# Cross attention: each head's norm ahead of the next head's maxima, and four output tiles taken head by head

## The chip, the core and the metric

The kernel runs on one core of a Trainium2 chip. Its time is the time of one execution on the device, in microseconds. The median of 3 runs of the kernel before is 2040.57 us (2038.38 to 2041.07).

The engines: PE multiplies matrices and writes to eight PSUM banks of 128 x 512 fp32 values; ACT (ScalarE) and DVE (VectorE) read those banks and write to SBUF; POOL (GpSimd) does a few small things; SP issues the weight transfers.

## The reference, cut to what matters

Two encoder layers, then two layers of another kind (not touched here). An encoder layer is an FFN, a mixer, a cross attention over a memory of 256 tokens, and a second FFN. The sequence has 256 tokens, D is 1024; the cross attention has 4 heads of 256.

```python
def memory_cross_attention(xn, memn, w_q, w_kv, w_o):
    B, S, D = xn.shape
    M = memn.shape[1]
    q = (xn @ w_q).reshape(B, S, XATTN_HEADS, XATTN_HEAD_DIM)
    k, v = jnp.split(memn @ w_kv, 2, axis=-1)
    k = k.reshape(B, M, XATTN_HEADS, XATTN_HEAD_DIM)
    v = v.reshape(B, M, XATTN_HEADS, XATTN_HEAD_DIM)
    s = jnp.einsum('bshd,bmhd->bhsm', q, k, preferred_element_type=F32) * (XATTN_HEAD_DIM ** -0.5)
    p = jax.nn.softmax(s, axis=-1).astype(v.dtype)
    o = jnp.einsum('bhsm,bmhd->bshd', p, v).reshape(B, S, D)
    return o @ w_o

# in a layer
h = h + memory_cross_attention(rms_norm(h, xattn_norm[l]), rms_norm(mem, mem_norm[l]),
                               xattn_w_q[l], xattn_w_kv[l], xattn_w_o[l])
h = h + 0.5 * swiglu_ffn(rms_norm(h, ffn2_norm[l]), ffn2_w_in[l], ffn2_w_out[l])
```

## The kernel before

Everything is kept with features on the 128 partitions and the 256 tokens along the free axis, so a 1024-wide vector is 8 tiles of 128 x 256 (`h`, `xs`, `yx`, `xo`). A big product splits both operands into a high part (fp32r) and the low rest: for each 128 x 128 weight block PE does three matmuls, weight high by x high, weight high by x low, weight low by x high (L383, L386, L387). An output tile is 8 blocks, 24 matmuls, and two tiles fill one bank.

The weights come in units of 8 blocks (512 KB) in the order in which PE takes them. SP loads them into a ring of 10 slots (L488); ACT writes a unit's high part (`w_hi`, 6 slots, L1031) and DVE its low part over the ring slot (`w_lo`, L1458). `s.ahead(u)` in the code of ACT and DVE makes the splits of all units up to some units past `u` at this place of the queue: up to u + 4 on ACT and u + 3 on DVE. ACT's split of a unit also waits until PE has begun the unit five before it (`unit_begun`). For the output projection of the cross attention (units U_XO to U_XO + 7) one unit is one output tile.

The order of the work is written out by hand for each engine, and the engines meet only at semaphores: `tell(name)` adds one, `need(name, n)` waits for n. Some names share a semaphore. In the cross attention (`cross_pe`, `cross_act`, `cross_dve`) a loop over i = 0 to 5 runs the heads as a pipeline. For head i:

- PE: the projection of the queries of head i + 1 (banks 1 to 3), the scores of head i (L753, bank 4 or 5), the transposes of the probabilities of head i - 1 (L767, bank 6), and the product of head i - 2's probabilities with the values (L778, bank 7). After the loop PE waits for `xo_lo` 4 and projects the output into banks 0, 1, 2 and 7, two tiles each.
- ACT: the copy of the queries (L1250), the exponentials of head i with their sums (L1263), the copy of the turned probabilities (L1270), the high part of head i - 2's output (L1274).
- DVE: the row maxima of head i and their scaling (L1751, L1753), the norm of head i - 1 (reciprocal of the sums and two multiplications, L1758, L1762), the low part of head i - 2's output (L1767).

Then `next_act` and `next_dve` add the output to `h` (L1502, as each bank is full: `w_full`), write the high and low parts of `xs` for the next FFN (L1061, L1468), and sum the squares (L1062, L1478 to L1486). The next FFN begins with `first_pair` (L448, L452, L453), which takes k-tiles 0 to 5 of its first two output tiles and then k-tiles 6 and 7 of both.

Of the kernel before, what the change touches and what calls it, by code (L numbers as in the profile page):

```python
# [25 lines left out]
ALU = mybir.AluOpType  # L26
AF = mybir.ActivationFunctionType
AX = mybir.AxisListType.X
# [18 lines left out]
XH = 4  # L47
# [130 lines left out]
def build_program(nc, counts, arrays, out):  # L178
    with ExitStack() as ctx:
# [559 lines left out]

        def cross_pe(pe, w):  # L740
            with pe.scope("cross"):
                first_pair(pe, w, yx, 0, "q_full")
                token_sums(pe, 6, wide=False)
                for i in range(XH + 2):
                    if i + 1 < XH:
                        project(pe, w, yx, KD, i + 1, "q_full")
                    if i < XH:
                        pe.e.wait_ge(*pe.need('q', i + 1))
                        if i >= 2:
                            pe.e.wait_ge(*pe.need('p', 2 * (i - 1)))  # L750
                        for t in range(2):
                            for d in range(2):
                                last = nc.tensor.matmul(bank[4 + i % 2][:, t * T:(t + 1) * T],  # L753
                                    qx[:, 2 * i + d, t * P:(t + 1) * P], kx[:, 2 * i + d, :], start=d == 0,
                                    stop=d == 1, skip_group_check=True)
                                if t == 1 and d == 1:
                                    last.then_inc(*pe.tell('s_full'))
                    if 1 <= i <= XH:
                        j = i - 1
                        pe.e.wait_ge(*pe.need('pn', 2 * j + 2))  # L760
                        if j:
                            pe.e.wait_ge(*pe.need('pt', j))
                        else:
                            pe.e.wait_ge(*pe.need('x_rstd', 1))
                        for t in range(2):
                            for m in range(2):
                                last = nc.tensor.transpose(bank[6][:, m * T + t * P:m * T + (t + 1) * P],  # L767
                                    px[:, j % 2, t * T + m * P:t * T + (m + 1) * P], ident)
                                if t == 1 and m == 1:
                                    last.then_inc(*pe.tell('t_full'))  # L770
                    if i >= 2:
                        j = i - 2
                        pe.e.wait_ge(*pe.need('pt', j + 1))
                        if j:
                            pe.e.wait_ge(*pe.need('xo_lo', j))
                        for d in range(2):
                            for m in range(2):
                                last = nc.tensor.matmul(bank[7][:, d * T:(d + 1) * T],  # L778
                                    vx[:, m, j * T + d * P:j * T + (d + 1) * P], ptx[:, j % 2, m * T:(m + 1) * T],
                                    start=m == 0, stop=m == 1, skip_group_check=True)  # L780
                                if d == 1 and m == 1:
                                    last.then_inc(*pe.tell('o_full'))
                pe.e.wait_ge(*pe.need('xo_lo', XH))
                for b in CROSS_BANKS:
                    project(pe, w, xo, KD, b, "w_full")

        def hybrid_pe(pe, w, l):
# [453 lines left out]
        def cross_act(a, s, l):  # L1241
            u0 = l * ENC_UNITS

            with a.scope("cross"):
# [10 lines left out]
                for i in range(XH + 2):  # L1255
# [15 lines left out]
                    if i >= 2:  # L1271
# [1 line left out]
                        a.e.wait_ge(*a.need('o_full', j + 1))  # L1273
                        nc.scalar.activation(hi(xo, 2 * j, 2), tiles(bank[7][:, :], 2),  # L1274
                            AF.Copy).then_inc(*a.tell('xo_hi'))
                next_act(a, s, xs, ENC(enc_par[:, l, :], "g_ffn2"), [u0 + U_XO + 2 * j + 2 for j in range(4)])

        def hybrid_act(a, s, l):
            u0 = DEC0 + l * DEC_UNITS
# [459 lines left out]
        def cross_dve(d, s, l):  # L1739
            u0 = l * ENC_UNITS  # L1740
            with d.scope("cross"):
                s.ahead(u0 + U_CROSS + 2)
                d.e.wait_ge(*d.need('x_rstd', 1))
                nc.vector.tensor_scalar(rs16[:, 0:2], rst[:, 0:4:2], 1.0 / 16, None, ALU.mult).then_inc(*d.tell())
                nc.vector.tensor_scalar(rs16[:, 2:4], rst[:, 0:4:2], -1.0 / 16, None, ALU.mult).then_inc(*d.tell())
                for i in range(XH + 2):
                    s.ahead(u0 + U_CROSS + 2 * min(i, 2) + 4)
                    if i < XH:
                        u = i % 2
                        d.e.wait_ge(*d.need('s_full', i + 1))  # L1750
                        nc.vector.reduce_max(mx[:, u, 0:2], tiles(bank[4 + u][:, :], 2), AX).then_inc(*d.tell())  # L1751
                        d.e.wait_ge(*d.own())
                        nc.vector.tensor_tensor(nm[:, u, 0:2], mx[:, u, 0:2], rs16[:, 2:4],  # L1753
                            ALU.mult).then_inc(*d.tell('mx'))
                    if 1 <= i <= XH:
                        j, u = i - 1, (i - 1) % 2
                        d.e.wait_ge(*d.need('p', 2 * j + 2))
                        nc.vector.reciprocal(sm[:, u, 2:4], sm[:, u, 0:2]).then_inc(*d.tell())  # L1758
                        d.e.wait_ge(*d.own())
                        for t in range(2):  # L1760
                            p = px[:, u, t * T:(t + 1) * T]
                            nc.vector.tensor_scalar(p, p, sm[:, u, 2 + t:3 + t], None,  # L1762
                                ALU.mult).then_inc(*d.tell('pn'))
                    if i >= 2:
                        j = i - 2
                        d.e.wait_ge(*d.need('xo_hi', j + 1))
                        nc.vector.tensor_tensor(lo(xo, 2 * j, 2), tiles(bank[7][:, :], 2),  # L1767
                            hi(xo, 2 * j, 2).bitcast(F32), ALU.subtract).then_inc(*d.tell('xo_lo'))
                next_dve(d, s, CROSS_BANKS, "w_full", 1.0, None, xs, ENC(enc_par[:, l, :], "g_ffn2"),
                    [u0 + U_XO + 2 * j + 2 for j in range(4)])  # L1770

        def hybrid_dve(d, w, l):
            par, u0 = dec_par[:, l, :], LAYERS * ENC_UNITS + l * DEC_UNITS
# [389 lines left out]
    return np.concatenate([first[0, :6], first[1, :6], first[0, 6:], first[1, 6:], blocks[2 * KD:]], 0)  # L2163


def gate_up(w):

    return np.concatenate([by_tile(w[:, :FF]).reshape(KF, KD, P, P), by_tile(w[:, FF:]).reshape(KF, KD, P, P)],
                          1).reshape(-1, P, P)


def encoder_blocks(i, l):
    w, kv = i["w_in"][l], i["xattn_w_kv"][l]
    return [pair_first(gate_up(i["ffn1_w_in"][l])), by_tile(i["ffn1_w_out"][l]),
            pair_first(by_tile(w[:, 0:1024])), by_row(w[:, 1024:1536]), by_tile(w[:, 1536:3584]),
            by_tile(kv[:, 0:D]), by_row(kv[:, D:D + 512]), by_row(kv[:, D + 512:]),
            by_tile(i["w_out"][l]), pair_first(by_tile(i["xattn_w_q"][l])), by_tile(i["xattn_w_o"][l]),
            pair_first(gate_up(i["ffn2_w_in"][l])), by_tile(i["ffn2_w_out"][l])]


# [68 lines left out]
```

## Time and profile before

| | |
|---|---|
| median of the timed runs | 2040.57 us |
| the profiled execution | 2038.23 us |
| its span in the trace | 2036.4 us |
| PE busy | 1941.9 us, 95% of the span |
| DVE busy | 1271.0 us, 62% |
| ACT busy | 968.9 us, 48% |
| PE, DVE, ACT in the chain that ended last | 88%, 7%, 2% |
| mean granted TensorE clock | 0.991 |

A row of the timeline is one instruction or a run of alike ones: start and length in us, engine, line, operation, tiles and shapes, and in brackets the idle time before it with what ended it. An fp32 matmul of L753 or L778 is recorded as two. A row of the windows gives a stretch, its length, the busy time of each engine (with instructions), the granted clock (1 is 2.4 GHz), and the busy share and rate of the DMA engines. The cross attention runs from about 460 to 532 us in layer 0 and from about 1171 to 1246 us in layer 1.

### The profile page before, as it was taken

How to read it: one execution, taken by the hardware profiler on the slowest of the kernel's cores; microseconds unless marked ns; L12 is line 12 of the kernel's file. 1: busy time of each engine (PE TensorE's matmuls, PEld its weight loads, DVE VectorE, ACT ScalarE, POOL GpSimd, SP SyncE). 2: the span in 40 equal slices, each digit the busy share in tenths (PEclk: the TensorE clock that was granted, in tenths of full speed). 3: DMA queues.
4: the chain of work that ended last, by engine and by line, in shares of the span. 5: the costliest groups of instructions: out<-in, count | busy, mean ns of one | idle time of the engine just before them, and what ended most of it. 6: DMA issues, size and time to landing. Idle time of an engine off the chain costs nothing.

```text
span 2036.4 us, 35117 instructions
## 1 busy us (share of the span) xinstructions
PE 1941.9 (95%) x14810; PEld 1804.3 (89%) x14810; DVE 1271.0 (62%) x2087; ACT 968.9 (48%) x1481; POOL 79.2 (4%) x68
## 2 busy tenths in 40 slices
PE   7999997988999999999979889999999999999999
PEld 7999995887999999999868879999988779988779
DVE  6766575454666567665843646665764778753776
ACT  5544555244544444455552445444553544643542
POOL 0000101300000000000013000000000000000000
PEclk9999998999999999999989999999999999999999
DMA  8555431222555655554312325555446325446222
GB/s 319 187 185 187 156 125 62 81 96 94 176 186 182 207 182 186 183 187 156 117 63 82 105 84 176 185 184 187 158 146 205 97 72 170 155 153 202 87 76 101
DMA packets 84461, 302.63 MB, mean 149 GB/s; under 512 B 9168, under 2 KB 11728, under 8 KB 84176
## 3 DMA queue, kind: packets, MB, share of 16 engines
q1 hardware_dynamic: 84304, 300.39, 44.4%
q8 instruction: 117, 1.92, 0.4%
q14 instruction: 40, 0.33, 0.1%
HBM read 299.30 MB, written 1.05 MB: 147 GB/s over the span
## 4 chain that ended last, share of the span: by engine, by line
PE 88%; DVE 7%; ACT 2%; issue 2%; DMA 0%; SPq 0%; DVEq 0%; ACTq 0%
PE bank L383 22%; PE bank L387 22%; PE bank L386 22%; PE bank L663 3%; PE bank L401 2%; PE bank L404 2%; PE bank L405 2%; DVE w_lo L1458 1%; PE bank L843 1%; PE bank L956 1%; PE bank L448 1%; PE bank L452 1%; PE bank L453 1%; PE bank L778 1%; PE bank L921 1%
## 5 line engine op out<-in xcount | busy, mean ns | idle before, releaser
L383 PE MATMUL bank<-xs,w_hi 128*128 128x256 f32 x2576 | 737.8, 286 | 4.1 <-issue 4.1
L387 PE MATMUL bank<-xs,w_lo 128*128 128x256 f32 x2576 | 724.6, 281 | 0.0
L386 PE MATMUL bank<-xs,w_hi 128*128 128x256 f32 x2576 | 724.5, 281 | 0.0
L1031 ACT ACTIVATE w_hi<-ring 128x1024 fp32r<-128x1024 f32 x544 | 565.4, 1052 | 330.8 <-PE bank L383 258.7
L1458 DVE TENSOR_TENSOR w_lo<-ring,w_hi 128x1024 fp32r<-128x1024 f32 x544 | 653.5, 1235 | 103.9 <-ACT w_hi L1031 103.0
L383 PEld LDWEIGHTS bank<-xs,w_hi 128*128 128x128 f32 x2576 | 487.9, 189 | 24.4 <-issue 20.5
L386 PEld LDWEIGHTS bank<-xs,w_hi 128*128 128x128 f32 x2576 | 487.9, 189 | 3.2 <-issue 2.9
L387 PEld LDWEIGHTS bank<-xs,w_lo 128*128 128x128 f32 x2576 | 487.7, 189 | 0.0
L383 PE MATMUL bank<-a,w_hi 128*128 128x256 f32 x704 | 196.9, 280 | 0.0
L387 PE MATMUL bank<-a,w_lo 128*128 128x256 f32 x704 | 196.6, 279 | 0.0
L386 PE MATMUL bank<-a,w_hi 128*128 128x256 f32 x704 | 196.4, 279 | 0.0
L387 PEld LDWEIGHTS bank<-a,w_lo 128*128 128x128 f32 x704 | 132.3, 188 | 0.0
L383 PEld LDWEIGHTS bank<-a,w_hi 128*128 128x128 f32 x704 | 132.0, 188 | 0.0
L386 PEld LDWEIGHTS bank<-a,w_hi 128*128 128x128 f32 x704 | 131.8, 187 | 0.0
L1533 DVE TENSOR_TENSOR arena<-bank,rstd 128x256 f32<-128x256 f32 x88 | 37.4, 425 | 148.4 <-PE bank L387 143.1
L1092 ACT ACTIVATE arena<-arena 128x256 f32<-128x256 f32 x88 | 36.8, 418 | 170.6 <-DVE arena L1533 170.6
L1374 ACT ACTIVATE arena<-arena 128x128 f32<-128x128 f32 x40 | 16.1, 402 | 97.2 <-DVE arena L1923 97.2
L1714 DVE TENSOR_TENSOR arena<-arena,bank 128x512 f32<-128x512 f32 x24 | 16.4, 685 | 58.6 <-PE bank L663 58.6
L1497 DVE SCALAR_TENSOR_TENSOR arena<-bank,rstd 128x512 f32<-128x512 f32 (+1 forms) x20 | 11.7, 583 | 61.8 <-PE bank L387 61.8
L1061 ACT ACTIVATE xs<-h,enc_par 128x256 fp32r<-128x256 f32 x40 | 18.5, 504 | 62.2 <-DVE h L1500 44.2
L448 PE MATMUL bank<-xs,w_hi 128*128 128x256 f32 x128 | 36.8, 287 | 10.2 <-DVE w_lo L1458 10.2
L401 PE MATMUL bank<-w_hi,xs 128*128 128x512 f32 (+2 forms) x128 | 43.9, 343 | 0.0
(398 smaller groups left out, 3138.6 us busy)
## 6 DMA issues: line engine op xcount, KB each, us to landing
ring<-in_w SPq DMA_DIRECT2D x560, 512.0 KB, 3.3
arena<-in_mem SPq DMA_DIRECT2D x2, 1024.0 KB, 12.9
const<-in_const SPq DMA_DIRECT2D x1, 1647.0 KB, 16.2
h<-in_x SPq DMA_DIRECT2D x1, 768.0 KB, 7.5
out<-h SPq DMA_DIRECT2D x3, 256.0 KB, 2.3
dec_par<-in_dec SPq DMA_DIRECT2D x1, 615.0 KB, 19.9
h<-in_x SPq DMA_DIRECT2D x1, 256.0 KB, 3.9
out<-h SPq DMA_DIRECT2D x2, 128.0 KB, 1.9
```

The lines of the kernel that those rows point to most:

```text
L383: last = nc.tensor.matmul(o, wh, hi(x, k0 + k), start=k == 0, stop=False, skip_group_check=True)
L386: nc.tensor.matmul(o, wh, lo(x, k0 + k), start=False, stop=False, skip_group_check=True)
L387: last = nc.tensor.matmul(o, wl, hi(x, k0 + k), start=False, stop=k == nk - 1, skip_group_check=True)
L401: last = nc.tensor.matmul(o, xh, wh, start=k == 0, stop=False, skip_group_check=True)
L404: nc.tensor.matmul(o, xl, wh, start=False, stop=False, skip_group_check=True)
L405: last = nc.tensor.matmul(o, xh, wl, start=False, stop=k == KD - 1, skip_group_check=True)
L448: last = nc.tensor.matmul(o, wh, hi(x, k), start=j == 0 and k == 0, stop=False, skip_group_check=True)
L663: last = nc.tensor.matmul(cut(bank[b], i), cut(lhs, c * GH + i), cut(rhs, c * GH + i), start=True, stop=True, skip_group_check=True)
L1031: nc.scalar.activation(w_hi[:, s * UNIT:(s + 1) * UNIT], ring[:, u % RU, :], AF.Copy).then_inc(sems("w_hi"), 1)
L1092: nc.scalar.activation(e, e, AF.Silu).then_inc(*a.tell('ff_e'))
L1458: nc.vector.tensor_tensor(w_lo[:, r * UNIT:(r + 1) * UNIT], ring[:, r, :], w_hi[:, s * UNIT:(s + 1) * UNIT].bitcast(F32), ALU.subtract).th ...
L1533: nc.vector.tensor_tensor(ebuf[:, f % 5, :], bank[f % 5][:, 0:T], rstd, ALU.mult).then_inc(*d.tell('g_r'))
```

## The change

Three parts, all within the cross attention of both layers. On DVE the norm of head i - 1 stands ahead of the maxima of head i in each step. On PE the first four of the eight output tiles (banks 0 and 1) are taken a head at a time: `early_output(j)` takes the two k-tiles of head j for all four tiles, as one weight unit; units 0 and 1 run in steps 4 and 5 of the loop, 2 and 3 after it, and the other four tiles then as before. The host lays these four units out by head (`by_head`). And the splits of the weights around the additions to `h` are asked for at other places: four units before the first addition, none before the second.

```diff
+                def early_output(j):
+                    pe.e.wait_ge(*pe.need('xo_lo', j + 1))
+                    for b in CROSS_BANKS[:2]:
+                        for half in range(2):
+                            o = bank[b][:, half * T:(half + 1) * T]
+                            for k in (2 * j, 2 * j + 1):
+                                wh, wl, first = w.two()
+                                last = nc.tensor.matmul(o, wh, hi(xo, k), start=half == 0 and k == 0, stop=False,
+                                    skip_group_check=True)
+                                if first:
+                                    last.then_inc(sems("unit_begun"), 1)
+                                nc.tensor.matmul(o, wh, lo(xo, k), start=False, stop=False, skip_group_check=True)
+                                last = nc.tensor.matmul(o, wl, hi(xo, k), start=False, stop=k == KD - 1,
+                                    skip_group_check=True)
+                        if j == XH - 1:
+                            last.then_inc(*pe.tell('w_full'))
...
                 for i in range(XH + 2):
...
+                    if i >= XH:
+                        early_output(i - XH)
                     if 1 <= i <= XH:
                         j = i - 1
                         pe.e.wait_ge(*pe.need('pn', 2 * j + 2))
...
-                pe.e.wait_ge(*pe.need('xo_lo', XH))
-                for b in CROSS_BANKS:
+                early_output(2)
+                early_output(3)
+                for b in CROSS_BANKS[2:]:
                     project(pe, w, xo, KD, b, "w_full")
...
-                next_act(a, s, xs, ENC(enc_par[:, l, :], "g_ffn2"), [u0 + U_XO + 2 * j + 2 for j in range(4)])
+                next_act(a, s, xs, ENC(enc_par[:, l, :], "g_ffn2"), [u0 + U_XO + n for n in (4, 4, 6, 8)])
...
                 for i in range(XH + 2):
                     s.ahead(u0 + U_CROSS + 2 * min(i, 2) + 4)
-                    if i < XH:
-                        u = i % 2
-                        d.e.wait_ge(*d.need('s_full', i + 1))
-                        nc.vector.reduce_max(mx[:, u, 0:2], tiles(bank[4 + u][:, :], 2), AX).then_inc(*d.tell())
-                        d.e.wait_ge(*d.own())
-                        nc.vector.tensor_tensor(nm[:, u, 0:2], mx[:, u, 0:2], rs16[:, 2:4],
-                            ALU.mult).then_inc(*d.tell('mx'))
                     if 1 <= i <= XH:
                         j, u = i - 1, (i - 1) % 2
                         d.e.wait_ge(*d.need('p', 2 * j + 2))
...
+                    if i < XH:
+                        u = i % 2
+                        d.e.wait_ge(*d.need('s_full', i + 1))
...
                     if i >= 2:
                         j = i - 2
                         d.e.wait_ge(*d.need('xo_hi', j + 1))
...
-                    [u0 + U_XO + 2 * j + 2 for j in range(4)])
+                    [u0 + U_XO + n for n in (4, 4, 6, 8)])
...
+def by_head(blocks):
+
+    first = blocks[:4 * KD].reshape(4, KD // 2, 2, P, P).transpose(1, 0, 2, 3, 4).reshape(-1, P, P)
+    return np.concatenate([first, blocks[4 * KD:]], 0)
...
-            by_tile(i["w_out"][l]), pair_first(by_tile(i["xattn_w_q"][l])), by_tile(i["xattn_w_o"][l]),
+            by_tile(i["w_out"][l]), pair_first(by_tile(i["xattn_w_q"][l])), by_head(by_tile(i["xattn_w_o"][l])),
```

The first place is DVE's queue from the maxima of head 1 to the norm of head 3, in layer 0. TENSOR_REDUCE and the TENSOR_TENSOR behind it are the maxima and their scaling, RECIPROCAL and TENSOR_SCALAR the norm, `xo<-bank,xo` the low part of a head's output, `w_lo` a split. Before:

```order
296 L1751 TENSOR_REDUCE arena<-bank 128x2
297 L1753 TENSOR_TENSOR arena<-arena 128x2
298 L1758 RECIPROCAL arena<-arena 128x2
299 L1762 TENSOR_SCALAR arena<-arena 128x256 x2
300 L1458 TENSOR_TENSOR w_lo<-ring,w_hi 128x1024 x2
301 L1751 TENSOR_REDUCE arena<-bank 128x2
302 L1753 TENSOR_TENSOR arena<-arena 128x2
303 L1758 RECIPROCAL arena<-arena 128x2
304 L1762 TENSOR_SCALAR arena<-arena 128x256 x2
305 L1767 TENSOR_TENSOR xo<-bank,xo 128x2x256
306 L1751 TENSOR_REDUCE arena<-bank 128x2
```

The same stretch after the change:

```order
296 L1772 RECIPROCAL arena<-arena 128x2
297 L1776 TENSOR_SCALAR arena<-arena 128x256 x2
298 L1781 TENSOR_REDUCE arena<-bank 128x2
299 L1783 TENSOR_TENSOR arena<-arena 128x2
300 L1479 TENSOR_TENSOR w_lo<-ring,w_hi 128x1024 x2
301 L1772 RECIPROCAL arena<-arena 128x2
302 L1776 TENSOR_SCALAR arena<-arena 128x256 x2
303 L1781 TENSOR_REDUCE arena<-bank 128x2
304 L1783 TENSOR_TENSOR arena<-arena 128x2
305 L1788 TENSOR_TENSOR xo<-bank,xo 128x2x256
306 L1772 RECIPROCAL arena<-arena 128x2
307 L1776 TENSOR_SCALAR arena<-arena 128x256 x2
```

The norm of a head has moved to before the maxima of the next one; the low part of head 0's output (305), which stood behind the norm of head 1, now stands between the maxima of head 2 and the norm of head 2.

The second place is PE's queue from the scores of head 2 to the output projection, in layer 0. `bank<-const,arena` are the transposes, `bank<-arena` scores or values, `xo` the output projection. Before:

```order
2993 L753 MATMUL bank<-arena 128x256 x4
2994 L767 MATMUL bank<-const,arena 128x128 x4
2995 L778 MATMUL bank<-arena 128x256 x4
2996 L753 MATMUL bank<-arena 128x256 x4
2997 L767 MATMUL bank<-const,arena 128x128 x4
2998 L778 MATMUL bank<-arena 128x256 x4
2999 L767 MATMUL bank<-const,arena 128x128 x4
3000 L778 MATMUL bank<-arena 128x256 x8
3001 L383 MATMUL bank<-xo,w_hi 128x256
```

After the change, from the second product with the values on (the rows left out at "..." are the other matmuls of two units of 24):

```order
2998 L798 MATMUL bank<-arena 128x256 x4
2999 L750 MATMUL bank<-xo,w_hi 128x256
3000 L754 MATMUL bank<-xo,w_hi 128x256
3001 L755 MATMUL bank<-xo,w_lo 128x256
...
3023 L787 MATMUL bank<-const,arena 128x128 x4
3024 L798 MATMUL bank<-arena 128x256 x4
3025 L750 MATMUL bank<-xo,w_hi 128x256
...
3049 L798 MATMUL bank<-arena 128x256 x4
3050 L750 MATMUL bank<-xo,w_hi 128x256
```

A unit of 24 matmuls of the output projection stands ahead of the transposes of head 3, and another ahead of the last product with the values.

The third place is DVE's queue behind the last low part of the output (`h` is the addition, `xs` the low part of the next input). Before:

```order
313 L1767 TENSOR_TENSOR xo<-bank,xo 128x2x256 x2
314 L1458 TENSOR_TENSOR w_lo<-ring,w_hi 128x1024 x2
315 L1502 SCALAR_TENSOR_TENSOR h<-bank,h 128x512
316 L1468 SCALAR_TENSOR_TENSOR xs<-h,enc_par,xs 128x256 x2
317 L1458 TENSOR_TENSOR w_lo<-ring,w_hi 128x1024 x2
318 L1502 SCALAR_TENSOR_TENSOR h<-bank,h 128x512
```

After the change, from the same place:

```order
313 L1788 TENSOR_TENSOR xo<-bank,xo 128x2x256 x2
314 L1479 TENSOR_TENSOR w_lo<-ring,w_hi 128x1024 x4
315 L1523 SCALAR_TENSOR_TENSOR h<-bank,h 128x512
316 L1489 SCALAR_TENSOR_TENSOR xs<-h,enc_par,xs 128x256 x2
317 L1523 SCALAR_TENSOR_TENSOR h<-bank,h 128x512
```

The two splits between the first and the second addition have moved to before the first.

## Rows read from the trace of the kernel before

**Rows 1.** The page's chain that ended last, by engine

```profile
PE 88%; DVE 7%; ACT 2%; issue 2%; DMA 0%; SPq 0%; DVEq 0%; ACTq 0%
```

**Rows 2.** Timeline of PE in the cross attention of layer 0

```profile
478.89 1.89 PE L753 MATMUL bank<-arena 128*128 128x256 f32 x8
...
482.48 0.66 PE L767 MATMUL bank<-const,arena 128*128 128x128 f32 x4 [1.71 <-DVE arena L1762]
...
488.58 1.89 PE L753 MATMUL bank<-arena 128*128 128x256 f32 x8
...
492.18 0.66 PE L767 MATMUL bank<-const,arena 128*128 128x128 f32 x4 [1.71 <-DVE arena L1762]
492.67 1.89 PE L778 MATMUL bank<-arena 128*128 128x256 f32 x8
494.40 1.89 PE L753 MATMUL bank<-arena 128*128 128x256 f32 x8
498.00 0.66 PE L767 MATMUL bank<-const,arena 128*128 128x128 f32 x4 [1.71 <-DVE arena L1762]
498.49 1.89 PE L778 MATMUL bank<-arena 128*128 128x256 f32 x8
502.52 0.66 PE L767 MATMUL bank<-const,arena 128*128 128x128 f32 x4 [2.14 <-DVE arena L1762]
503.01 1.89 PE L778 MATMUL bank<-arena 128*128 128x256 f32 x8
506.41 1.97 PE L778 MATMUL bank<-arena 128*128 128x256 f32 x8 [1.50 <-DVE xo L1767]
509.79 0.38 PE L383 MATMUL bank<-xo,w_hi 128*128 128x256 f32 x1 [1.41 <-DVE xo L1767]
```

**Rows 3.** Timeline of ACT, same stretch

```profile
487.12 0.55 ACT L1263 ACTIVATE arena<-bank,arena 128x256 f32<-128x256 f32 x1
...
488.20 0.59 ACT L1270 ACTIVATE arena<-bank 128x512 f32<-128x512 f32 x1
...
491.43 0.56 ACT L1263 ACTIVATE arena<-bank,arena 128x256 f32<-128x256 f32 x1 [2.05 <-DVE arena L1753]
...
494.60 0.60 ACT L1274 ACTIVATE xo<-bank 128x512 fp32r<-128x512 f32 x1 [1.13 <-PE bank L778]
```

**Rows 4.** Timeline of DVE, from the low parts to the next FFN

```profile
501.05 0.69 DVE L1767 TENSOR_TENSOR xo<-bank,xo 128x512 fp32r<-128x512 f32 x1 [3.11 <-ACT xo L1274]
...
515.75 0.69 DVE L1502 SCALAR_TENSOR_TENSOR h<-bank,h 128x512 f32<-128x512 f32 x1 [3.15 <-PE bank L387]
...
517.82 2.35 DVE L1458 TENSOR_TENSOR w_lo<-ring,w_hi 128x1024 fp32r<-128x1024 f32 x2
...
521.40 0.69 DVE L1502 SCALAR_TENSOR_TENSOR h<-bank,h 128x512 f32<-128x512 f32 x1 [1.22 <-PE bank L387]
...
524.27 2.35 DVE L1458 TENSOR_TENSOR w_lo<-ring,w_hi 128x1024 fp32r<-128x1024 f32 x2
...
527.05 0.69 DVE L1502 SCALAR_TENSOR_TENSOR h<-bank,h 128x512 f32<-128x512 f32 x1 [0.43 <-PE bank L387]
...
530.38 2.35 DVE L1458 TENSOR_TENSOR w_lo<-ring,w_hi 128x1024 fp32r<-128x1024 f32 x2
...
532.71 0.76 DVE L1502 SCALAR_TENSOR_TENSOR h<-bank,h 128x256 f32<-128x256 f32 x2
...
533.71 0.89 DVE L1468 SCALAR_TENSOR_TENSOR xs<-h,enc_par,xs 128x256 fp32r<-128x256 f32 x2 [0.25 <-ACT xs L1061]
```

**Rows 5.** Timeline of PE, the last product with the values in layer 1

```profile
1218.49 3.62 PE L778 MATMUL bank<-arena 128*128 128x256 f32 x8 [1.50 <-DVE xo L1767]
```

**Rows 6.** Windows: layer 0 from s1, layer 1 from T3, layer 0's projection

```profile
478.89:509.79 30.90, 20.72 (x122) 17.21 (x121) 10.50 (x25) 11.46 (x24) 0.00 (x0) 1.00 0.11 35
1213.70:1223.53 9.83, 6.91 (x21) 4.80 (x21) 1.44 (x3) 1.79 (x3) 0.00 (x0) 0.65 0.00 0
509.79:532.51 22.72, 22.72 (x193) 22.72 (x193) 15.43 (x20) 12.15 (x17) 0.00 (x0) 1.00 0.54 182
```

More of the change, by code:

```diff
@@ L1763, in cross_dve @@
                                 ALU.mult).then_inc(*d.tell('pn'))
+                    if i < XH:
+                        u = i % 2
+                        d.e.wait_ge(*d.need('s_full', i + 1))
+                        nc.vector.reduce_max(mx[:, u, 0:2], tiles(bank[4 + u][:, :], 2), AX).then_inc(*d.tell())
+                        d.e.wait_ge(*d.own())
+                        nc.vector.tensor_tensor(nm[:, u, 0:2], mx[:, u, 0:2], rs16[:, 2:4],
+                            ALU.mult).then_inc(*d.tell('mx'))
                     if i >= 2:
```

## The prediction

> **What bounds the kernel now.** I read the page's chain first: PE holds 88% of it, DVE 7%, ACT 2% [rows 1]. So the kernel is a stream of matmuls, and time can be won only where PE stands still or runs at the lower clock. Then I read PE's timeline through the cross attention of layer 0, because the change touches nothing else. With s for scores, T for the transposes of the probabilities and PV for probabilities times values, [rows 2] give s1 at 478.89, T0 at 482.48, s2 at 488.58, T1 at 492.18, PV0 at 492.67, s3 at 494.40, T2 at 498.00, T3 at 502.52, PV3 at 506.41, and the projection of the output at 509.79. Every T and the last two rows carry an idle time released by DVE. From start to start a group of s or PV takes 494.40 - 492.67 = 1.73 us when the next is ready, a T 0.49 us.
>
> The third view is the ACT and DVE timelines of the same stretch. T1 waits for the norm of head 1, whose exponentials begin on ACT at 487.12 and take 1.08 us (the next ACT row is at 488.20) [rows 3]: before s2 begins. The norm is late only because it stands in DVE's queue behind the maxima of s2. Last come the windows: in layer 0 the granted clock is 1.00 through the tail and through the eight output tiles, which take 22.72 us, 2.84 us a tile. In layer 1 the stretch from T3 to the projection has a mean granted clock of 0.65 (a fall from 2.4 to 1.2 GHz for a part of it), and takes 9.83 us against 509.79 - 502.52 = 7.27 in layer 0 [rows 2, 6]; PV3 there is 3.62 us long [rows 5] against 1.97 [rows 2].
>
> **The change, part by part, in layer 0.** No matmul, transfer or split is added or removed: the same 24 matmuls per weight unit, in another order.
>
> Norm ahead of maxima. Each PE step starts when the one before has issued, if DVE is in time.
> - T0 can start at 478.89 + 1.73 = 480.62, 1.86 earlier. From T0 to s2 (T0 and the last query projection) is 488.58 - 482.48 = 6.10, so s2 is at 486.72.
> - T1 at 486.72 + 1.73 = 488.45. Its exponentials move earlier with PE's steps, by 1.86, to 485.26, and end at 486.34; the norm takes less than 1 us on DVE (from the start of a low part to the transposes behind its norm it is 1.47, below, and 0.6 of that is the low part), so it is done near 487.3, 1.1 us to spare. T1 gains 3.73 in all. PV0 is then at 488.94, s3 at 490.67, and its issue ends at 492.40.
> - T2 is not free. The low part of head 0's output now stands between the maxima of s2 and the norm of head 2. ACT has the exponentials of head 2 at s2 + 2.85 (491.43 - 488.58) = 489.57, the copy of the turned probabilities at 490.65, and the high part of head 0 after another 0.58 [rows 3], at 491.23, later than PV0 + 1.93 (494.60 - 492.67) = 490.87. DVE's low part follows 0.63 later (2.56 after PV in all: 501.05 against 498.49), at 491.86, and the transposes start 1.47 after such a low part (502.52 - 501.05) [rows 2, 4]: T2 at 493.33. So 0.93 us of stall remain; its bounds are 0 (if the queue were free) and 1.87 (the whole old wait: 498.00 less 494.40 + 1.73). I take 0.93, since each piece is a row.
>
> Early tiles. They take the first four output tiles a head at a time, one weight unit for each head.
> - PV1 is at 493.82, the first unit starts at 495.55 and ends at 498.39. Its wait is for the low part of head 0, done near 492.5; behind it in PE's queue stand T3 and PV2, and they don't wait for it. Meanwhile DVE does the maxima of s3, the low part of head 1 (ACT's high part about 495.8, so 496.4) and the norm of head 3, T3 ready near 497.9. T3 at 498.39, PV2 at 498.88.
> - Second unit at 500.61, PV3 at 503.45: both stalls on DVE before PV3 and the projection fall into units. PV2 + 2.56 puts the low part of head 2 at 501.4, 2 us before PV3 wants it. Third unit 505.18, fourth 508.02 (low part of head 3: 506.0, done 506.6), and the remaining four tiles start at 510.86.
> - Before, they would start at 509.79 + 11.36 = 521.15. Gain: 10.29 us.
>
> The switches between bank and bank inside a unit I cost at 0: the kernel's first projections already change the accumulator inside a unit. From below it cannot gain, and from above I allow 0.1 us for each of 16 switches, 1.6 us a layer, the bound being the 0.12 us spacing of one matmul (22.72 / 192).
>
> Weights. The four units of the early tiles have their low parts made before s2, in the old order too, so PE need not wait. The next four are now split in one go after the low part of head 3: 506.6 + 4 x 1.17 = 511.3 (2.33 for two, 530.38 to 532.71), the first of them ready at 507.8 for 510.86. What is late next is the tail of DVE: h0 at 511.3, h1 2.07 later at 513.4, then 2.87 to the next two splits, h2 at 518.6 (its bank full at 516.5), 3.33 and two splits more, h3 at 524.25, 2.0 us after the projection's end at 522.22; now it is 0.20 after (532.71 against 532.51) [rows 4, 6]. The next FFN's first pair covers this: it takes six k-tiles of both halves first, 36 matmuls or 4.26 us, so it needs the low part of tile 6 at 526.48, and gets it at 524.25 + 1.00 + 0.45 = 525.7. Slack 0.8 us, so 0 in the sum, but it is thin. The DMA queue has room: 35 GB/s in the tail [rows 6].
>
> Layer 1 has the same rows plus the clock's loss, 9.83 - 7.27 = 2.56 us. Its fall came after a run of stalls in which PE did little; with the stalls filled I take it as gone. If it stays the term is 0; if layer 0 got one as well it is 0 too (2.56 lost, 2.56 kept).
>
> **Sum.** 2 x 10.29 + 2.56 = 23.1 us. The profiled execution took 2038.23, which gives 2015.1. The median of the timed runs is 2.34 us above it, close to one more fall of the clock, which the change would also remove; otherwise it stays on top, 2017.4. I say 2016.
>
> **Rivals.**
> - DVE's tail is the new bound. If DVE is 2 us later than worked out, h3 passes the slack by 1.2 in each layer, and the sum of squares behind it delays the FFN's norm as well: 2 to 4 us in all, 2017 to 2019. For it: the slack of 0.8; against it: ACT and DVE rows here are regular to 0.1 us. Chance 0.13.
> - The norms stay late from T1 on (exponentials held behind the splits on ACT, or low parts in front). Then only T0 and what the units cover is won. That is the stall before T3, 502.52 - (498.49 + 1.73) = 2.30, before PV3, 506.41 - (503.01 + 1.73) = 1.67, and before the projection, about 1.60: 1.86 + 5.57 = 7.43 a layer, 2 x 7.43 + 2.56 = 17.4 with the clock: 2020.8. Against it: the row at 487.12. Chance 0.08.
> - The clock's fall stays or moves: 2015.1 + 2.6 = 2017.7, twice 2020.3. Chance 0.08.
> - The change doesn't do what it says: the low part of head 0 or the units are not ready in time, and the early tiles run after the last head in effect. Then the norms alone give 1.86 + 1.87 + 0.94 = 4.67 a layer, 2 x 4.67 + 2.56 = 11.9: 2026.3. Against it: 3 us of slack on each. Chance 0.03.
> - Slower: the clock goes down in the mixed stretch of T, PV and short units and stays down through the projection. Eight tiles at half the clock cost 22.7 us more in each layer: 2038.2 - 20.6 + 45.4 = 2063. Any other length decides in proportion: half a microsecond for each at 1.2 GHz, slower than before from about 46 us of them in sum. Against it, layer 0 kept 1.00 with more idle time, and layer 1 was back at 2.4 GHz before the projection. Chance 0.02.
>
> The Trainium skill (TensorE: Matmul & The Clock Gate, "A second HAM failure mode: psum-queue depth-cycling") tells of a kernel that went round its PSUM banks with brief idles between groups of matmuls and swung between the two clock levels. That is the shape of the new stretch, and speaks for the last rival; by its rule the time would come out above 2038. The trace agrees that such a mixed stretch can lose the clock [rows 6], but in one layer of two and with more idle time than remains.
>
> **How the numbers follow.** Forecast 0.66, the rivals 0.34 as given. A measurement of this kernel tells about 0.2%, 4 us, from no change. All but the last case lie beyond it; from the last but one, whose gain of 11.9 could shrink, I give 0.01 to no change: faster 0.97, same 0.01, slower 0.02. The range takes in the gain of the T2 stall (2 x 0.93) and a better clock elsewhere below, to 2011, and the first three rivals above, the switches (3.2) or the median's 2.3 on top, to 2022.
>
> **What would show it.** In the profile after: T0 and T1 right behind the scores with no wait on DVE; a wait of about 0.9 before T2; none before T3, PV3 and the projection; 32.0 us from s1 to the fifth output tile in both layers; granted clock 1.00 there in both layers; no wait in the first pair of the second FFN. A wait of over 0.3 us before the first pair's last k-tiles, or a clock below 1 in the units, would make the forecast wrong.

## The result and the profile after

The changed kernel takes 2018.41 us in the median of 4 runs (2014.68 to 2022.55), against 2040.13 before in the same session: ratio 0.9895, 95% interval 0.9871 to 0.9919, 21.7 us faster. 2016 was forecast, in a range of 2011 to 2022. The profiled execution took 2022.55, with a span of 2020.8 us, 15.6 less than the span of before.

The page of the changed kernel, chain by engine; PE holds a point more of it than in [rows 1]:

```profile
PE 89%; DVE 7%; ACT 2%; issue 2%; DMA 0%; DVEq 0%; SPq 0%
```

PE's timeline in the cross attention of layer 0, which answers to [rows 2] (L771 scores, L787 transposes, L798 values):

```profile
478.83 1.89 PE L771 MATMUL bank<-arena 128*128 128x256 f32 x8
...
480.56 0.60 PE L787 MATMUL bank<-const,arena 128*128 128x128 f32 x4
...
486.60 1.89 PE L771 MATMUL bank<-arena 128*128 128x256 f32 x8
488.32 0.60 PE L787 MATMUL bank<-const,arena 128*128 128x128 f32 x4
488.76 1.89 PE L798 MATMUL bank<-arena 128*128 128x256 f32 x8
490.49 1.89 PE L771 MATMUL bank<-arena 128*128 128x256 f32 x8
493.13 0.66 PE L787 MATMUL bank<-const,arena 128*128 128x128 f32 x4 [0.75 <-DVE arena L1776]
493.62 1.89 PE L798 MATMUL bank<-arena 128*128 128x256 f32 x8
...
498.19 0.60 PE L787 MATMUL bank<-const,arena 128*128 128x128 f32 x4
...
503.18 1.89 PE L798 MATMUL bank<-arena 128*128 128x256 f32 x8
```

T0 and T1 follow the scores at once. One wait is left of six, 0.75 us before T2. Between 493.62 and 498.19, and again from 498.62 to 503.18, stands a unit of the output projection where PE stood still.

DVE's timeline there and at the tail, which answers to [rows 4] (L1788 the low part, L1772 and L1776 the norm, L1479 a split, L1523 the addition to h):

```profile
491.66 0.69 DVE L1788 TENSOR_TENSOR xo<-bank,xo 128x512 fp32r<-128x512 f32 x1 [2.25 <-ACT xo L1295]
492.26 0.15 DVE L1772 RECIPROCAL arena<-arena 128x2 f32<-128x2 f32 x1
492.46 0.62 DVE L1776 TENSOR_SCALAR arena<-arena 128x256 f32<-128x256 f32 x2
...
506.34 4.62 DVE L1479 TENSOR_TENSOR w_lo<-ring,w_hi 128x1024 fp32r<-128x1024 f32 x4
510.88 0.69 DVE L1523 SCALAR_TENSOR_TENSOR h<-bank,h 128x512 f32<-128x512 f32 x1
...
523.67 0.75 DVE L1523 SCALAR_TENSOR_TENSOR h<-bank,h 128x256 f32<-128x256 f32 x2
```

The norm of head 2 waits in the queue for the low part of head 0, and h3, the last addition to `h`, comes at 523.67, 1.81 us after the next FFN's first row at 521.86 (0.20 before).

PE in the second FFN of layer 1, which has no counterpart in layer 0 (L448 is the first pair, L461 the token sums behind it):

```profile
1224.10 0.28 PE L448 MATMUL bank<-xs,w_hi 128*128 128x256 f32 x1
...
1227.44 0.39 PE L448 MATMUL bank<-xs,w_hi 128*128 128x256 f32 x1 [1.42 <-DVE xs L1489]
...
1231.42 0.59 PE L461 MATMUL bank<-ssum,const 128*128 128x256 f32 x2
```

Here the first pair takes 7.32 us to the token sums; in layer 0 it takes 5.63 (521.86 to 527.49). So 1.69 us are given back.

The windows of the changed kernel, both cross attentions from first pair to first pair, and a stretch in the last of the four layers (the last three columns: granted clock, DMA share, GB/s):

```profile
459.80:521.86 62.06, 61.31 (x470) 59.20 (x469) 34.50 (x60) 34.21 (x59) 0.00 (x0) 1.00 0.40 136
1162.04:1224.10 62.06, 61.31 (x471) 59.20 (x470) 34.50 (x60) 34.23 (x59) 0.00 (x0) 1.00 0.41 136
1800.00:1810.00 10.00, 10.00 (x57) 9.86 (x58) 3.37 (x7) 5.33 (x12) 4.08 (x6) 0.66 0.32 106
```

The cross attention took 72.71 us in layer 0 and 75.23 in layer 1 before (459.80 to 532.51, 1171.02 to 1246.25), so it gained 10.65 and 13.17. The two profiled executions then compare as follows, by the start of each stage:

| stretch | after less before, us |
|---|---|
| cross attention, layer 0 | -10.65 |
| cross attention, layer 1 | -13.17 |
| first pair of layer 1's second FFN | +1.7 |
| first FFN and mixer of layer 0 | 0.0 (-1.3, +1.3) |
| mixer of layer 1 | +1.7 |
| rest of layer 1's second FFN | +1.2 |
| last two layers | +3.6 |
| sum (span) | -15.6 |

Only the first three rows are the change's: the two cross attentions and the wait right behind one of them. The last two layers have the same instructions in both kernels; a granted clock of 0.66 over 10 us stands there in this trace. The 1.2 and 1.3 us of the FFN rows are taken up at the end of the part on the prediction.

### The profile page after: what moved, and what is told of

The parts are those of the page before. It is cut to its first block, busy times and chain, and to the rows that moved or that the text cites. A ratio compares the mean times of both kernels' runs of the same rounds, so it can differ in the third digit from the quotient of the medians.

```text
span 2020.8 us, 35123 instructions
## 1 busy us (share of the span) xinstructions
PE 1944.4 (96%) x14810; PEld 1811.1 (90%) x14810; DVE 1270.5 (63%) x2087; ACT 967.6 (48%) x1481; POOL 79.2 (4%) x68
## 4 chain that ended last, share of the span: by engine, by line
PE 89%; DVE 7%; ACT 2%; issue 2%; DMA 0%; DVEq 0%; SPq 0%
PE bank L383 22%; PE bank L387 21%; PE bank L386 21%; PE bank L663 3%; DVE w_lo L1479 2%; PE bank L401 2%; PE bank L405 2%; PE bank L404 2%; PE bank L864 1%; PE bank L448 1%; PE bank L452 1%; PE bank L453 1%; PE bank L977 1%; PE bank L942 1%; PE bank L837 1%
## 5 line engine op out<-in xcount | busy, mean ns | idle before, releaser
L1479 DVE TENSOR_TENSOR w_lo<-ring,w_hi 128x1024 fp32r<-128x1024 f32 x544 | 652.6, 1234 | 101.9 <-ACT w_hi L1052 101.1
L448 PE MATMUL bank<-xs,w_hi 128*128 128x256 f32 x128 | 37.2, 290 | 11.6 <-DVE w_lo L1479 10.2
L383 PE MATMUL bank<-ms,w_hi 128*128 128x256 f32 x128 | 39.3, 307 | 5.8 <-DVE w_lo L1479 5.8
```

What stands on the lines that cost most here:

```text
L383: last = nc.tensor.matmul(o, wh, hi(x, k0 + k), start=k == 0, stop=False, skip_group_check=True)
L448: last = nc.tensor.matmul(o, wh, hi(x, k), start=j == 0 and k == 0, stop=False, skip_group_check=True)
L1479: nc.vector.tensor_tensor(w_lo[:, r * UNIT:(r + 1) * UNIT], ring[:, r, :], w_hi[:, s * UNIT:(s + 1) * UNIT].bitcast(F32), ALU.subtract).th ...
```

## The experiments

Each median is compared with runs of the kernel before on the same chip in the same session, so the figure for before differs a little from one to the next. All figures "from first pair to first pair" are read as above.

**Norm alone** (e1). The kernel before with this one edit (here and in the diffs below, a block of lines of DVE's loop is given by its name in parentheses, and cut code by "..."):

```diff
                 for i in range(XH + 2):
                     s.ahead(u0 + U_CROSS + 2 * min(i, 2) + 4)
-                    (maxima of head i)
-                    (norm of head i - 1)
+                    (norm of head i - 1)
+                    (maxima of head i)
                     (low part of head i - 2)
```

> The kernel before with one part of the change alone: on DVE the norm of head i - 1 stands ahead of the maxima of head i. By the prediction's steps T0 is 1.86 us earlier, T1 3.73, T2 4.67, and the projection 4.6 us earlier in each layer, 9.3 us in all, about 2031 us. If the clock's fall in layer 1 needs the stalls that remain, it stays (2031); if it goes too, 2028. Rival (norms late from T1 on): only 1.9 us a layer, 2036.

Measured: 2030.38 us against 2039.12, ratio 0.9957 (0.9943 to 0.9970). PE in layer 0 (L753, L767, L778 as in the kernel before; L1755 is the norm):

```profile
485.90 1.89 PE L753 MATMUL bank<-arena 128*128 128x256 f32 x8
487.62 0.60 PE L767 MATMUL bank<-const,arena 128*128 128x128 f32 x4
488.06 1.89 PE L778 MATMUL bank<-arena 128*128 128x256 f32 x8
489.79 1.89 PE L753 MATMUL bank<-arena 128*128 128x256 f32 x8
492.42 0.66 PE L767 MATMUL bank<-const,arena 128*128 128x128 f32 x4 [0.74 <-DVE arena L1755]
492.92 1.89 PE L778 MATMUL bank<-arena 128*128 128x256 f32 x8
496.94 0.66 PE L767 MATMUL bank<-const,arena 128*128 128x128 f32 x4 [2.14 <-DVE arena L1755]
497.44 1.89 PE L778 MATMUL bank<-arena 128*128 128x256 f32 x8
500.83 1.97 PE L778 MATMUL bank<-arena 128*128 128x256 f32 x8 [1.50 <-DVE xo L1767]
504.21 0.39 PE L383 MATMUL bank<-xo,w_hi 128*128 128x256 f32 x1 [1.41 <-DVE xo L1767]
```

T1 has no wait, T2 0.74, and the three stalls behind are what they were in [rows 2]. From first pair to first pair layer 0 took 67.78 us, 4.9 less than 72.65 (a cross attention of the kernel before with no fall of the clock, below). Layer 1 took 69.46, 1.68 more, with a fall of the granted clock to half for 3.4 us from its T3 on (1203 us): with the late stalls still there the clock can still go. The rival of late norms is out.

**Tiles alone** (e2). The changed kernel with the norm behind the maxima, where it was (so the early tiles and the moved splits stay):

```diff
-                    (norm of head i - 1)
-                    (maxima of head i)
+                    (maxima of head i)
+                    (norm of head i - 1)
```

> The changed kernel with the norm behind the maxima as before: only the early tiles. By the steps they cover the stalls before T3, PV3 and the projection, 5.6 us a layer; the three waits of 1.7 us before T0, T1 and T2 stay. 11.2 us, and the clock's 2.6 on top, less 1.7 for the wait in the first pair of layer 1's second FFN: about 2028 us. Rival (the early tiles cost something by their switches between banks): a unit takes over 2.84 us from start to start and the gain is smaller, 4 us a layer or less.

Measured: 2030.66 us against 2039.12, ratio 0.9953 (0.9940 to 0.9966). PE in layer 0:

```profile
480.25 0.66 PE L787 MATMUL bank<-const,arena 128*128 128x128 f32 x4 [1.71 <-DVE arena L1783]
...
489.95 0.66 PE L787 MATMUL bank<-const,arena 128*128 128x128 f32 x4 [1.71 <-DVE arena L1783]
...
495.77 0.66 PE L787 MATMUL bank<-const,arena 128*128 128x128 f32 x4 [1.71 <-DVE arena L1783]
496.26 1.89 PE L798 MATMUL bank<-arena 128*128 128x256 f32 x8
...
500.82 0.60 PE L787 MATMUL bank<-const,arena 128*128 128x128 f32 x4
501.26 1.89 PE L798 MATMUL bank<-arena 128*128 128x256 f32 x8
```

The three early waits stay, the late ones are gone; from 496.26 to 500.82 go a PV and a unit, 4.56 us or 1.73 + 2.83, so the switches between banks cost nothing. 66.73 and 66.78 us in the two layers, 5.9 less than 72.65. The two parts add up: 4.9 + 5.9 = 10.8, and both together gave 10.6. The median is 8.5 us under the kernel before, where 12.1 were expected (11.2 and 2.6, less 1.7). The trace puts none of the missing 3.6 us into the cross attentions or the first pairs. Part of it is the 2.6 us for the clock, which b1 and b2 below show to be too much, and this trace has falls of the clock in the last two layers.

**The kernel before, twice more** (b1, b2), unchanged.

> The kernel before, for a second trace of it. The question is whether the falls of the clock in the last two layers (at 1500 to 1510, 1790 to 1810 and 2010 to 2025 us in the traces of the changed kernels, up to 3.9 us each, none in the one trace of the kernel before) come with the change or by chance. By chance: here at least one of these three places shows a granted clock under 0.99. With the change: none does. And whether the fall in the cross attention of layer 1 (1215 to 1222 us, 2.56 us) belongs to the old order: then it shows in one of the two layers here, where the six traces with the early tiles have none in either.

> The kernel before a third time, with the same two questions as the run beside it: a granted clock under 0.99 in the last two layers says that those falls have nothing to do with the change; one in a cross attention says that the stalls of the old order cost the clock now and then.

The windows of b1 (layer 0's cross attention, its part from T3 to the projection, layer 1's cross attention, a stretch in the last layer):

```profile
458.20:533.42 75.22, 65.04 (x470) 60.36 (x469) 36.60 (x61) 35.10 (x59) 0.00 (x0) 0.95 0.34 113
500.88:510.71 9.83, 6.91 (x21) 4.87 (x21) 1.44 (x3) 1.79 (x3) 0.00 (x0) 0.65 0.01 2
1173.59:1246.24 72.65, 62.47 (x470) 58.75 (x469) 36.59 (x61) 35.10 (x59) 0.00 (x0) 1.00 0.36 117
1815.00:1825.00 10.00, 10.00 (x71) 9.80 (x71) 3.37 (x7) 3.68 (x11) 3.04 (x4) 0.83 0.28 93
```

Here the fall is in layer 0 and layer 1 has none; b2 has it in neither (72.60 and 72.66 us). Falls in the last two layers are in both. So those belong to the program, not to the change, and the first trace of before had none by chance. In the old order 3 of 8 cross attentions (four traces, three of the kernel before and that of e6, below) had the clock at half for 6.8 us, which cost 2.6 us each, and with the norm alone (e1) 1 of 2 had it for 3.4 us. With the early tiles there was none in 18 (nine traces).

**fgain apart** (e3, and e6 on the kernel before). The name fgain shares a semaphore with x_lo. Both edits are

```diff
-              ... fgain="x_lo",
+              ... fgain="mixed",
```

> The changed kernel with the product for the final norm (fgain) counted on another semaphore than x_lo. Theory S: in layer 1 PE waits 1.42 us in the first pair of the second FFN because DVE's fgain adds to the count of x_lo before that FFN begins, so each k-tile waits for the low part of the next one, and the eighth for fgain itself. With a count of its own the wait is gone: 0 instead of 1.42 us at the first pair in layer 1, token sums 5.6 us after the pair's start instead of 7.3, total 1.7 us faster than the changed kernel. Rival D: DVE is simply late in layer 1; then the wait stays at 1.4 us.

> The kernel before with fgain counted on another semaphore than x_lo. In its trace the token sums of layer 1's second FFN come 5.77 us after the first pair's start, in layer 0 5.64: if the shared count was there all along and nearly hidden by the early h of the old order, it is 5.63 here in layer 1 too, 0.13 us less, where the changed kernel lost 1.69 by the same cause. If it stays at 5.77, the 0.13 has another cause.

In e3's trace the wait is gone:

```profile
1226.31 0.28 PE L448 MATMUL bank<-xs,w_hi 128*128 128x256 f32 x1
...
1231.94 0.59 PE L461 MATMUL bank<-ssum,const 128*128 128x256 f32 x2
```

5.63 us instead of 7.32, though DVE's h3 comes as late as in the changed kernel (1.81 us after the first pair began). The count was the cause and the late h3 the condition. In DVE's code fgain stands between the eighth low part and the FFN and adds one to x_lo. PE's waits are counted back from the total with it, so in layer 1 PE asks at each k-tile for one low part more than it needs. Its wait of 1.42 us is before the sixth k-tile of the first tile, which then needs the low part of the seventh. In e6 the same stretch took 5.64, against 5.77 in before, 5.73 in b1 and 5.72 in b2: the old order all but hid it.

```profile
1245.30 0.28 PE L448 MATMUL bank<-xs,w_hi 128*128 128x256 f32 x1
...
1250.94 0.59 PE L461 MATMUL bank<-ssum,const 128*128 128x256 f32 x2
```

The time does not show the 1.7 us that were expected: e3 took 2020.76 us (0.9892 to 0.9922 of before), the changed kernel beside it 2019.61 (0.9888 to 0.9915). Its trace has a mean granted clock of 0.989 against 0.991, and 1.7 us are less than what the stages outside the change vary by from run to run.

**Low part later** (e4). The changed kernel with the low part of head i - 3 between norm and maxima in step i, and one more step:

```diff
-                for i in range(XH + 2):
+                for i in range(XH + 3):
...
                     (norm of head i - 1)
+                    if i >= 3:
+                        (low part of head i - 3)
                     (maxima of head i)
-                    if i >= 2:
-                        (low part of head i - 2)
```

> The changed kernel with the low part of a head's output one step later on DVE, behind the norm of the head after next. Theory: the 0.75 us that PE still waits before T2 come from this low part standing ahead of the norm in DVE's queue. Then T2 starts right behind s3 (no wait), every step behind it is 0.85 us earlier in each layer, 1.7 us in all. Rival: the wait comes from the exponentials of head 2 on ACT, which start only 2.85 us after the scores; then T2 still waits by 0.5 us or more and the gain is under 0.5 us a layer.

Measured: 2016.09 us, ratio 0.9881 of before (0.9864 to 0.9897), 3.5 us under the changed kernel beside it, where 1.7 were expected and the intervals overlap. PE, then DVE, in layer 0 (L1781 is the low part in this kernel):

```profile
489.94 1.89 PE L771 MATMUL bank<-arena 128*128 128x256 f32 x8
491.67 0.60 PE L787 MATMUL bank<-const,arena 128*128 128x128 f32 x4
492.11 1.89 PE L798 MATMUL bank<-arena 128*128 128x256 f32 x8
```

```profile
490.13 0.17 DVE L1772 RECIPROCAL arena<-arena 128x2 f32<-128x2 f32 x1 [1.27 <-ACT arena L1284]
490.33 0.62 DVE L1776 TENSOR_SCALAR arena<-arena 128x256 f32<-128x256 f32 x2
491.11 0.69 DVE L1781 TENSOR_TENSOR xo<-bank,xo 128x512 fp32r<-128x512 f32 x1 [0.15 <-ACT xo L1295]
```

T2 follows the scores with no wait. 60.94 us in each layer, 1.0 less than the 61.96 of the changed kernel on the same chip (e0, below). Here the norm follows the exponentials at once and ends before 491.1, in time for T2 at 491.67; so the exponentials were not what held it.

**Splits at the old places** (e7).

```diff
-                next_act(... [u0 + U_XO + n for n in (4, 4, 6, 8)])
+                next_act(... [u0 + U_XO + 2 * j + 2 for j in range(4)])
```

and the same for next_dve.

> The changed kernel with the splits of the weights asked for at the old places (two before each addition to h instead of four, none, two, two). DVE then waits for bank 0 between its splits, about 0.9 us, and h3 comes 1.2 us later than in the changed kernel (3.0 instead of 1.8 us after the projection's end). The slack in layer 0's first pair (0.96 us by the trace) is passed: a wait of 0.2 to 0.4 us there, and 2.6 instead of 1.42 us in layer 1, 1.5 us slower in all. Rival: the moved splits do nothing, since DVE has as much to do before h3 in either order; then layer 0 has no wait and layer 1 1.42.

Measured: 2018.62 us, 0.9889 of before (0.9868 to 0.9911). PE in layer 1, then DVE's h3 there:

```profile
1220.56 0.28 PE L448 MATMUL bank<-xs,w_hi 128*128 128x256 f32 x1
...
1224.64 0.39 PE L448 MATMUL bank<-xs,w_hi 128*128 128x256 f32 x1 [2.16 <-DVE xs L1489]
```

```profile
1223.11 0.75 DVE L1523 SCALAR_TENSOR_TENSOR h<-bank,h 128x256 f32<-128x256 f32 x2
```

h3 comes 2.55 us after the first pair's start instead of 1.81: the moved splits are worth 0.74 us of DVE's tail, not 1.2. Layer 0 still hides it (5.65 us to the token sums), layer 1 waits 2.16 instead of 1.42. So this third part gains 0.75 us, where 1.5 were expected, all of it in the layer with the shared count.

**Both edits** (e5, e9), and the changed kernel beside them (e0, e8).

> The changed kernel once more, as the base for the runs beside it and to see where the two groups of its times (about 2015 and 2022 us) come from. Theory A: they differ by falls of the clock outside the cross attention (in the profiled execution one at 1801 to 1808 us, in the second of the last two layers, cost 3.9 us by the shift against the kernel before). Then the times again lie between 2014 and 2023, and from s1 to the end of the projection both cross attentions are 10.5 to 13.2 us shorter than before in this trace too, whatever the total is. Rival: the cross attention itself varies, with a granted clock below 1 in it; then the shift over these stretches differs from the first trace by over 1 us.

> Both edits together, the candidate for the fastest kernel: 1.7 us from the wait in layer 1 and 1.7 us from T2 in both layers, 3.4 us faster than the changed kernel, about 2012 to 2019 us by the clock's luck. If the two share a cause in DVE's tail the sum is smaller: the low part moved later would push the splits and h3 later and bring back a wait in the first pair.

> The changed kernel again, beside the fastest variant on the same chip: 2015 to 2022 us, both cross attentions 62.0 us from first pair to first pair, a wait of 1.42 us in the first pair of layer 1's second FFN, no granted clock under 0.99 in either cross attention.

> The variant with both edits again. By the traces it does 3.6 us less work on the path than the changed kernel (1.0 in each cross attention, 1.69 in the first pair of layer 1). If that is all that differs, its median lies 3.6 us below that of the run beside it, give or take 2 us for the clock's falls elsewhere; the first time it was 2.2. Rival: the gain is given back elsewhere, and the medians are within 1 us.

| | changed kernel | both edits |
|---|---|---|
| first session (e0, e5), median, ratio to before | 2019.61, 0.9888 to 0.9915 | 2017.42, 0.9877 to 0.9906 |
| second session (e8, e9) | 2020.26, 0.9893 to 0.9927 | 2016.13, 0.9870 to 0.9910 |
| cross attention, layers 0 and 1 (e0, e5) | 61.92, 61.96 | 60.98, 60.94 |
| first pair to token sums, layer 1 | 7.32 | 5.63 |

The windows of e5, both cross attentions:

```profile
462.10:523.08 60.98, 60.98 (x470) 59.17 (x469) 34.78 (x60) 34.13 (x59) 0.00 (x0) 1.00 0.42 139
1161.70:1222.64 60.94, 60.94 (x471) 59.13 (x470) 34.85 (x60) 34.14 (x59) 0.00 (x0) 1.00 0.43 139
```

PE is busy for the whole of both stretches: nothing is left to win there by order. e0's four executions stay within 2018.9 and 2020.1, so the spread of the first four (2014.7 to 2022.6) was not seen again there; its cross attentions are 10.7 us below 72.65 in both layers. The medians lie 2.2 and 4.1 us below those of the changed kernel, about the 3.6 us of the traces, but the intervals of the ratios overlap, so the kernel with both edits has the least work on PE's path by these stretches, and is only probably faster than the changed kernel by its times. The times don't set it above e4, which has the later low part alone: e4's median in the same session was 2016.09, and its trace has the shortest span of all, 2010.1.

## Why the prediction was right

The mechanism was the one foreseen, with one step wrong in layer 1 and one term mis-sized.

- *Norm ahead.* T0 and T1 came at 480.56 and 488.32 (480.62 and 488.45 worked out). The wait before T2 was 0.75 us by the row, 0.91 by the starts (493.13 less 490.49 + 1.73), against 0.93, and e4 showed its cause to be the one named.
- *Early tiles.* T3 at 498.19 for 498.39, PV3 at 503.18 for 503.45, the end of the projection at 521.86 for 522.22. e2 confirmed a price of 0 for the switches between banks.
- *Sum of the layer.* 10.65 measured for 10.29; e1 and e2 show 4.9 and 5.9 for its parts, where 4.67 and 5.57 were worked out. Part of the small excess is that a T with no wait before it takes 0.44 us to the next start (488.32 to 488.76) instead of the 0.49 read from T that had waited, and the stretch from T0 to s2 takes 6.04 instead of 6.10. From s1 to the fifth output tile it was 31.7 us in both layers, where 32.0 was foretold.
- *The clock.* The 2.56 us of layer 1 went, and no fall was seen in 18 cross attentions with the early tiles. But as a term of the median it was mis-sized: in the kernel before a fall comes in 3 of 8, about 1 us per layer on average by these few traces, not always one in layer 1. That the one profiled execution of before had just one such fall, and none in the last two layers, was chance, so the base of 2038.23 was one too. The rival of a clock that stays down did not come about: with the early tiles all 18 stretches were at 1.00.
- *DVE's tail.* h3 was foreseen at 2.0 us after the projection's end and came at 1.81; the slack in the first pair held in layer 0. The step that failed is "layer 1 has the same rows": by a semaphore count shared with fgain it needs each low part one k-tile earlier, so the slack was not there, and 1.69 us were lost. This is the first rival's mechanism, in one layer, by another cause than a late DVE. It is also what the prediction itself gave as a sign against it, a wait of over 0.3 us in the first pair.
- *The median.* 2018.4 for 2016.0. 1.69 of the difference is that wait. By all the traces the change is worth about 21.4 us (an estimate: 2 x 10.6, and 1.9 for the falls in two layers, less 1.7), where the sum had 23.1, and the medians give 21.7. That they agree to 0.3 us is partly luck, since the changed kernel's 12 runs lie between 2014.7 and 2024.2. The stages outside the change make that spread, and which one made it in which run can't be said, since only the profiled runs have a trace.

The 1.2 and 1.3 us in the FFNs of the table are not the change's. Runs of one kernel differ in them as much: the second FFN of layer 1, from its first pair to the next stage, took 188.0 us in before and b1 and 186.6 in b2, and, less the 1.69 us of the wait, 189.2 in the changed kernel's first trace and 186.5 in e0 and e8. The difference is no step; it grows evenly over the FFN's long first product. The changed kernel in its first trace, then in e0:

```profile
1260.00:1340.00 80.00, 80.00 (x669) 80.00 (x669) 52.40 (x84) 34.00 (x42) 0.00 (x0) 1.00 0.58 183
1260.00:1340.00 80.00, 80.00 (x684) 80.00 (x683) 53.49 (x88) 35.22 (x44) 0.00 (x0) 1.00 0.57 186
```

At the same granted clock of 1.00 PE begins 669 matmuls in one and 684 in the other, 120.0 and 117.3 ns apart (117.3 in e8 and b2 too, 118.7 in before and b1), with no wait recorded. What sets the spacing stays open.

## What to carry to other kernels

When one engine's queue serves several steps of a pipeline, put first what is ready first: here the norm of the last head was ready before the scores of the next, and the order alone was worth 4.9 us a layer and a further 1.0 when the low part went behind the norm as well. A projection whose input arrives in pieces can be cut by input piece, with all output tiles open, and its units set into the stalls of the chain that makes the pieces; switching accumulators cost nothing here. When work ahead gets faster, check the slack of what stands behind it layer by layer, with the counts of shared semaphores, not only the instructions: a wait for one signal too many cost about 0.1 us until the producer came later, and 1.7 us then.

## What the runs showed of the hardware

The granted clock can fall to half in a mixed stretch although the same stretch keeps it in another execution of the same program: the stretch from T3 to the projection was at 1.00 in layer 0 and 0.65 in layer 1 in one trace, and the other way round in the next (9.83 against 7.27 us). With the early tiles in it, it did not fall in 18 such stretches, though in two of them (e2) the three early waits of 1.71 us were still there.

In the last two layers falls of 3.4 or 6.8 us come and go, at about 1505 and 1800 to 1820 us, and once at 1915 (e2). One at 1800.7 in the changed kernel's first trace lasts 6.8 us and moves what follows it by 3.0 us against the kernel before, with PE busy throughout. The falls near 2020 us begin after the last instruction or within its last 1.5 us. The mixers of both layers have falls in every trace, too.

Even at a granted clock of 1.00 and with no wait recorded, the same matmuls of 256 columns started at different spacings in executions of one kernel: 120.0 or 117.3 ns between 1260 and 1340 us of the changed kernel, 118.7 or 117.3 there in the kernel before. All this sets the spread of this kernel's times: among the three traces of the changed kernel the second FFN of layer 1 differs by up to 2.7 us, the mixer of layer 1 by 2.7 and the last two layers by 2.0. A gain of 1.7 us (e3) does not show in the median of five runs beside it.
